# A three-block network on one core: norms, gated sums, head norms and HGRN levels written out anew between the matmul stages

## The reference, cut to what matters

```python
def rmsnorm(x, w):
    y = x32 * lax.rsqrt(jnp.mean(x32 * x32, axis=-1, keepdims=True) + EPS)
    return (y * w.astype(jnp.float32)).astype(x.dtype)

def second_block(...):                      # NSA, then FoX
        h = rms_norm(x, norm_g[i, 0])
        x = x + rms_norm(m, norm_g[i, 1])
        h = rms_norm(x, norm_g[i, 2])
        x = x + rms_norm(squared_relu_mlp(h, mlp_w_up[i], mlp_w_down[i]), norm_g[i, 3])

def hgrn2_chunkwise(q, k, log_f, v):
        bc = jnp.cumsum(gc, axis=2)
        diff = bc[:, :, :, None, :] - bc[:, :, None, :, :]
        decay = jnp.exp(jnp.where(mask[:, :, None], diff, NEG))
        a = jnp.einsum('bhtd,bhsd,bhtsd->bhts', qc, kc, decay)
        o = (jnp.einsum('bhtd,bhdv->bhtv', qc * jnp.exp(bc), s_st)
             + jnp.einsum('bhts,bhsv->bhtv', a, vc))

def hgrn2_mixer(h, w_in, lb, norm_w, w_out):
    o = merge_heads(head_rmsnorm(o, norm_w)).astype(h.dtype) * jax.nn.silu(g)
    return o @ w_out

def third_block(...):                       # mLSTM, then HGRN
        x = x + gate1 * y                   # y: the mixer's output
        hn = rmsnorm(x, norm2_w[layer]) * (1 + scale2) + shift2
        x = x + gate2 * y                   # y: SwiGLU, then the experts
    return rmsnorm(x, final_norm_w)
```

## Time and profile before

| what | us |
|---|---|
| median of 3 runs (lowest, highest) | 3282.08 (3279.73, 3282.49) |
| the profiled execution | 3282.36 |
| its span, first to last instruction | 3280.6 |
| PE busy | 2953.2 (90%) |
| DVE busy | 2152.5 (66%) |
| ACT busy | 1558.9 (48%) |
| POOL busy | 103.0 (3%) |

### The profile page before, as it was taken

One profiled execution on the slowest core, in us unless ns is written; L12 is line 12 of the kernel. 1 busy time (PEld: TensorE's weight loads), 2 busy tenths in 40 slices (PEclk: granted clock), 3 DMA queues, 4 the chain that ended last, 5 costly groups with the idle time before them and its releaser, 6 DMA issues. The chain is left out here.

```text
span 3280.6 us, 48259 instructions
## 1 busy us (share of the span) xinstructions
PE 2953.2 (90%) x19343; PEld 2606.9 (79%) x19343; DVE 2152.5 (66%) x3308; ACT 1558.9 (48%) x2454; POOL 103.0 (3%) x131
## 2 busy tenths in 40 slices
PE   7897998899999997878989699888997679999997
PEld 6896876679999997647978599768986669999996
DVE  5456498666666665275664666666555858888887
ACT  3442313344444444264443544544344248787875
POOL 0000000000000000200000000000001200000000
PEclk9998999999999998888999899899998879999998
DMA  6443488765665554304434244424552049998894
GB/s 262 157 180 140 154 354 341 311 226 193 207 224 208 202 194 163 129 1 153 180 142 154 77 180 158 158 84 154 179 193 103 1 165 337 332 339 326 326 339 185
DMA packets 76827, 648.61 MB, mean 198 GB/s; under 512 B 6104, under 2 KB 31192, under 8 KB 34032
## 3 DMA queue, kind: packets, MB, share of 16 engines
q1 hardware_dynamic: 49584, 621.09, 50.7%
q10 hardware_dynamic: 27072, 25.17, 2.4%
HBM read 632.60 MB, written 13.63 MB: 197 GB/s over the span
## 5 line engine op out<-in xcount | busy, mean ns | idle before, releaser
L1190 PE MATMUL ps<-x_hi,up_hi 128*128 128x256 f32 x1632 | 461.1, 283 | 2.8 <-DVE up_lo L1281 2.7
L1193 PE MATMUL ps<-x_lo,up_hi 128*128 128x256 f32 x1632 | 460.1, 282 | 0.0
L1194 PE MATMUL ps<-x_hi,up_lo 128*128 128x256 f32 x1632 | 460.0, 282 | 0.0
L346 DVE TENSOR_TENSOR weight_lo<-ring,weight_hi 128x1024 fp32r<-128x1024 f32 x236 | 288.1, 1234 | 258.4 <-ACT weight_hi L339 250.4
L339 ACT ACTIVATE weight_hi<-ring 128x1024 fp32r<-128x1024 f32 x236 | 245.6, 1054 | 184.7 <-PE ps L516 119.2
L1286 DVE TENSOR_TENSOR down_lo<-ring,down_hi 128x1024 fp32r<-128x1024 f32 x182 | 222.8, 1224 | 166.1 <-ACT down_hi L1243 166.1
L1190 PEld LDWEIGHTS ps<-x_hi,up_hi 128*128 128x128 f32 x1632 | 311.9, 191 | 10.3 <-DVE up_lo L1281 3.4
L1193 PEld LDWEIGHTS ps<-x_lo,up_hi 128*128 128x128 f32 x1632 | 312.0, 191 | 6.8
L1194 PEld LDWEIGHTS ps<-x_hi,up_lo 128*128 128x128 f32 x1632 | 311.6, 191 | 0.0
L1243 ACT ACTIVATE down_hi<-ring 128x1024 fp32r<-128x1024 f32 x182 | 193.1, 1061 | 232.2 <-PE ps L1215 232.2
L494 PE MATMUL ps<-x_hi,weight_hi 128*128 128x256 f32 x1024 | 291.5, 285 | 8.8 <-DVE weight_lo L346 8.1
(11 more groups left out here) (517 smaller groups left out, 6345.1 us busy)
## 6 DMA issues: line engine op xcount, KB each, us to landing
ring<-in_stream SPq DMA_DIRECT2D x181, 2048.0 KB, 7.7
ring<-in_experts SPq DMA_DIRECT2D x121, 1536.0 KB, 8.6
ring<-in_stream SPq DMA_DIRECT2D x22, 1536.0 KB, 6.4
gates<-kept_gates ACTq DMA_DIRECT2D x12, 1024.0 KB, 8.8
kept_gates<-away_first ACTq DMA_DIRECT2D x8, 768.0 KB, 10.7
kept_gates<-away_last ACTq DMA_DIRECT2D x8, 768.0 KB, 9.3
params_mix<-in_mix SPq DMA_DIRECT2D x1, 3072.0 KB, 21.6
params_ln<-in_ln SPq DMA_DIRECT2D x2, 1024.0 KB, 5.4
```

The source lines that it names most:

```text
L346: dve.tensor_tensor(self.place(self.lo, b), self.raw(b), self.place(self.hi, b), ALU.subtract).then_inc(self.split, 1)
L1190: last = pe.matmul(out, hi[:, o:o + P], x_hi[:, k, :], start=(k == 0), stop=False)
L1193: pe.matmul(out, hi[:, o:o + P], x_lo[:, k, :], start=False, stop=False)
L1194: last = pe.matmul(out, lo[:, o:o + P], x_hi[:, k, :], start=False, stop=(k == DK - 1))
```

## The change

The pieces above are written anew.

- Layer norms: the sum of x comes out of the adding instruction, tile by tile; ScalarE sums the squares of the centred x (center) while VectorE multiplies (norm_rows). The parameters of the second one are loaded at the start of the feed-forward ahead of it, those of the last norm in the stage ahead of it. The second one also squares x for the next stage, so that the NSA projection no longer does.
- post_norm: VectorE multiplies y with the gain while ScalarE squares it, for the first 512 columns as soon as the first of the two chunks of a mixer's output projection is done, and one instruction then multiplies with the root and adds to x.
- add_gated behind a mixer works on the first 512 columns likewise, and squares x in halves.
- HeadNorm: the weight of the norm goes into the scale with which the transposed result is copied, so GpSimd no longer multiplies; VectorE works head by head, one product from PSUM to each tile, and splits the head before the last two; the weight blocks' low parts stand between them.
- hgrn2: logarithm and cumulative sum move ahead of the last chunks, and the decays of levels 0 and 1 and the scaling of level 0 go into the projection. Of levels 0, 1 and 2, ScalarE copies the results straight to their places (weight_far, and squares of 64 and 32 tokens), and TensorE streams at levels 1 and 2 only the query columns that are needed; levels from 3 on stream whole tiles and are placed by VectorE under a mask, as all were. GpSimd clears the halves that no level has written yet.
- The output is stored in two DMAs, tile by tile.
- The four PSUM banks of y are in the order tile, half (they were in the order half, tile).

```diff
--- x squares, layer norm (both)
-            act.activation(junk[:, t, :], x[:, t, :], ACT.Square, accum_out=x_squares[:, t:t + 1])
+        def mean_square(act, out, of, to):
+            return act.activation(out, of, ACT.Square, scale=D ** -0.5, accum_out=to)
+        def center(act, mean_ready, junk, squared):
+            for t in range(TT):
+                act.wait_ge(mean_ready, t + 1)
+                act.activation(junk(t), halves(x[:, t, :]), ACT.Square, bias=less_mean[:, t:t + 1],
+                               accum_out=squares[:, t, 0:1]).then_inc(squared, 1)
+        def norm_rows(dve, z, g, b, mean_ready, squared, var_ready, rstd_ready, weighed, normed):
+            for t in range(TT):
+                dve.wait_ge(mean_ready, t + 1)
+                dve.scalar_tensor_tensor(z[:, t, :], x[:, t, :], less_mean[:, t:t + 1], g, ALU.add, ALU.mult).then_inc(weighed, 1)
+                dve.wait_ge(squared, t + 1)
+                dve.tensor_scalar(spare[:, t:t + 1], squares[:, t, 0:1], 1.0 / D, LN_EPS, ALU.mult, ALU.add).then_inc(var_ready, 1)
+            for t in range(TT):
+                dve.wait_ge(weighed, t + 1)
+                dve.wait_ge(rstd_ready, t + 1)
+                dve.scalar_tensor_tensor(x[:, t, :], z[:, t, :], rstd[:, t:t + 1], b, ALU.mult, ALU.add).then_inc(normed, 1)
--- feed_forward(..., ahead=(buf_2[:], d["ln2"])); add_gated(gate(3), ahead=(buf_last[:], d["last"]))
+                    if ahead is not None:
+                        sp.dma_start(*ahead).then_inc(ahead_loaded, 16)
--- post_norm, VectorE
-                    variances(dve, squares, var_ready, squared)
+                        dve.wait_ge(n_ready, 1)
+                        dve.tensor_tensor(weighed_y[:, :, 0:WIDE], bank_n(0), spread(g[:, 0:WIDE], 1, TT), ALU.mult).then_inc(y_weighed, 1)
+                        dve.wait_ge(n_ready, 2)
+                    for t in (1, 0):
+                        if t == 0:
+                            dve.wait_ge(squared, 1)
+                            variance(dve, squares, 0, square_parts).then_inc(var_ready, 1)
...
                     for t in range(TT):
                         dve.wait_ge(rstd_ready, t + 1)
-                        if t > 0:
-                            dve.wait_ge(x_ready, t)
-                        dve.scalar_tensor_tensor(halves(scaled_y[:]), y_banks(t), rstd[:, t:t + 1], halves(g), ALU.mult,
-                                                 ALU.mult).then_inc(y_scaled, 1)
-                        dve.wait_ge(y_scaled, t + 1)
-                        dve.tensor_tensor(x[:, t, :], x[:, t, :], scaled_y[:], ALU.add).then_inc(x_ready, 1)
+                        dve.scalar_tensor_tensor(x[:, t, :], weighed_y[:, t, :], rstd[:, t:t + 1], x[:, t, :], ALU.mult,
+                                                 ALU.add).then_inc(x_ready, 1)
--- add_gated with a mixer, VectorE
+                        o = slice(0, WIDE)
+                        dve.wait_ge(n_ready, 1)
+                        dve.tensor_tensor(gated_y[:, :, o], bank_n(0), spread(gate[:, o], 1, TT), ALU.mult).then_inc(y_gated, 1)
+                        dve.wait_ge(y_gated, 1)
+                        dve.tensor_tensor(x[:, :, o], x[:, :, o], gated_y[:, :, o], ALU.add).then_inc(x_ready, 1)
+                        o = slice(WIDE, D)
                         dve.wait_ge(n_ready, 2)
+                        for t in range(TT): ...
--- HeadNorm
+                weights.low(dve, 1)
                 dve.wait_ge(self.rstd_ready, 1)
-                dve.tensor_tensor(heads(self.o[:]), heads(self.o[:]), spread(self.var[:], 3, P), ALU.mult).then_inc(self.normed, 1)
+                for h in range(HEADS_C + 2):
+                    if h < HEADS_C:
+                        o = slice(h * P, h * P + P)
+                        for t in range(TT):
+                            last = dve.scalar_tensor_tensor(self.o[:, t, o], ps[:, 4 + 2 * t + h // 4, h % 4 * P:h % 4 * P + P],
+                                                            self.var[:, t, h:h + 1], self.gate[:, t, o], ALU.mult, ALU.mult)
+                        last.then_inc(self.normed, 1)
+                    b = h - 2
+                    if b >= 0:
+                        dve.wait_ge(self.high_ready, b + 1)
+                        dve.scalar_tensor_tensor(self.parts[1][:, b, :], ps[:, b % 4, 0:TOKENS], col("head_w", self.first_w + b),
+                                                 self.parts[0][:, b, :], ALU.mult, ALU.subtract).then_inc(self.ready, 1)
+                        if b in (1, 3, 5):
+                            weights.low(dve, b // 2 + 2)
...
-                pool.tensor_tensor(self.gate[:], self.gate[:], spread(self.norm_w, 1, TT), ALU.mult).then_inc(self.weighed, 1)
--- hgrn2, VectorE in the projection
+                    step(last)
+                    keep(1)
+                    decays(dve, 0).then_inc(diff_ready, 1)
+                    weights.low(dve, 29)
+                    dve.wait_ge(exped, 1)
+                    scale_q(dve, 0)
+                    weights.low(dve, 30)
+                    scale_k(dve, 0).then_inc(scaled, 1)
+                    weights.low(dve, 31)
+                    keep(2)
+                    dve.wait_ge(scaled, 1)
+                    decays(dve, 1).then_inc(diff_ready, 1)
+                    weights.low(dve, 32)
+                    keep(3)
+                    pool.memset(k_dec[0][:, :, P:TOKENS], 0.0)
+                    pool.memset(q_dec[0][:, :, 0:P], 0.0)
--- hgrn2, the levels
+                        pool.memset(weight[:], 0.0).then_inc(zeroed, 1)
+                        pool.memset(split(q_dec[1][:], P // 2)[:, :, 0, :], 0.0)
+                        pool.memset(split(k_dec[1][:], P // 2)[:, :, 1, :], 0.0).then_inc(zeroed, 1)
+                            if n > PLAIN:
+                                place(n - 1)
+                                    for o in range(0, P, 2 * half):
+                                        last = act.activation(weight[o:o + half, t, 4 * b:4 * b + 4, o + half:o + 2 * half],
+                                                              got[o:o + half, :, o + half:o + 2 * half], ACT.Copy)
+                                    if 0 < n < 3:
+                                        out, q_t = (a.rearrange("p (g a w) -> p g a w", a=2, w=levels[n])[:, :, 1, :] for a in (out, q_t))
+                                    m = levels[1] if n == 1 else P
+                                    last = pe.matmul(out[0:m], k[:, h, s * P:s * P + m], q_t, start=True, stop=True)
--- the end
-                sp.dma_start(d["out"], x[:]).then_inc(stored, 16)
+                    for t in range(TT):
+                        sp.wait_ge(normed, t + 1)
+                        sp.dma_start(d["out"][:, t, :], x[:, t, :]).then_inc(stored, 16)
```

462 lines of the change are left out of this document (250 added, 212 removed).

## The result

The changed kernel takes 3249.14 us (median of four runs, 3247.82 to 3250.10) against 3281.54 for the kernel before on the same chip (3279.73 to 3282.49): a ratio of 0.990, 95% interval 0.9884 to 0.9919. The interval leaves out 1, so the gain of one per cent is clear of noise. 3249.5 was forecast, in a range of 3240 to 3262. The profiled execution took 3248.25 us, its span 3246.5 (before 3280.6).

What follows compares the result with a forecast made beforehand. TensorE is busy nine tenths of the span, so time is won only where it waits, at stage changes and in HGRN. Terms sum to -32.7 from 3282.36, giving 3249.7, median 0.28 lower: 3249.5 us, range 3240 to 3262.

Steps and rivals of the forecast that it cites:

- -1.9: First layer norm: TensorE's gap of 9.30 us falls to 7.3 as ScalarE squares beside VectorE; 1.9 us less.
- -5.4: Second layer norm: earlier parameter DMA and x squared in the same stage let the next weight split end 5.4 us sooner.
- -2.6: Gated sums behind two mixers: half-width operations and a half square cut 6.1 us to 3.4; 2.6 us less each.
- each post norm: Norms behind NSA and FoX: first half weighed and squared beside the second chunk's matmuls; 3.1 us less each.
- Rival 4: Norm stretches: fused products or accumulating sums 1 us slower than separate ones in each of eight, 3257 us; chance 0.08.
- The head norm: Two head norms: a loss of 1.5 us each from the order and root lock, plus 1.6 each from cold clock.
- Rival 1: Head norm doesn't lose: GpSimd's root isn't held up and transposes keep the clock up, 3243 us; chance 0.17.
- HGRN: Projection and levels: moved work stalls the projection but lets levels start sooner, weighted sum at 2586.4; 14.7 us less.
- Rival 2: HGRN's overfull projection costs more: each of the last seven blocks stalls another 1.2 us, 3258 us; chance 0.20.
- Rival 3: Broken work leaves TensorE at 1.2 GHz: 14 blocks cancel the gain, all 32 give 3326 us; chance 0.02.
- The clearings: Early clearings of q_dec and k_dec beside VectorE's scaling of x: a loss of 0.5 us, bounds 0 to 1.9.
- The tail: Last norm and output: parameters a stage earlier and the second output half with half the bytes; 2.5 us less.

Runs made afterwards that it cites:

- e3: Changed kernel, but in both head norms VectorE makes the first weight_lo behind its wait for GpSimd's root, not beside it: 3247.12 us (one run).
- e1: Changed kernel with only HGRN's projection and levels as before the change: 3262.57 us, ratio 0.9941.
- e9: Changed kernel, head norm order untouched, plus 70 unread transposes at the start of each of the two head norm stages: 3250.49 us (one run).
- e6: Changed kernel with the exchanges of e4 and e5 and e2's dense head norm order, first weight_lo before the root wait, six transpose banks: 3231.60 us.
- e10: Kernel of e6 with 72 unread transposes ahead of the first real one in each head norm: 3227.94 us, ratio 0.9835.
- e4: Changed kernel with the last weight block's high part ahead of the second exponential on ScalarE in HGRN's projection: 3245.94 us, ratio 0.9891.
- e5: Changed kernel, ScalarE taking level 2's exponential before the far-half copies and GpSimd clearing q_dec and k_dec halves only after the input splits: 3254.60 us (one time).
- e8: The changed kernel once more, nothing altered: 3251.24 us, ratio 0.9906.
- e2: Changed kernel with gate products beside the root, then root products in two halves and dense transposes in both head norms: 3243.05 us, ratio 0.9884.

## Why the prediction was right

**The bound, and the norms.** Every stage change was read as a chain of single instructions, and the chains came out as added up: -1.96 for -1.9, -5.3 for -5.4, -2.4 and -2.55 for -2.6. The largest miss is 0.4 for each post norm, the second root beside a fused product with inputs in SBUF. The prediction priced such a lock in the head norm, where e3 shows it, and overlooked it here, where no run takes the product away. No run undid these edits one by one either. e1, which keeps them all, is 18.6 us faster than the kernel before (3281.15 and 3262.57), where the ledger gives its edits 16.8. Rival 4 (accumulating and fused forms slower by 1 us a stretch) is out: 0.08 for an accumulator on VectorE, 1.28 for a fused product.

**The head norm.** It loses, as forecast, by 3.5 and 3.9 where 3.1 was said. The order, the lock on the root included, cost 2.2 and 2.9 until the first matmul (1.5 said; the lock in it was 0.90 for 1.2), and the cold start the rest, 1.3 and 1.0 (1.6 said): the matmuls ran 2.8 and 2.1 us at half clock. So the 3.1 said lies near the 3.5 measured with one part too small and the other too large. Five traces with this head norm end its stages 40.2 to 40.9 and 39.7 to 41.1 us after the squares, so both losses are known to about 1 us only. Rival 1, no loss, falls. The reason given for the clock was incomplete: the prediction held it to be low because of the gap and to stay low in broken work. e9 shows that broken work is enough by itself. Nor do show that dense transposes bring the clock up within 3.24 us, as the prediction reads them: in e6 sixteen dense ones needed 5.8 and 6.0. What the prediction didn't ask is whether the old large products with the norm's weight in the copies' scale would be better still. e6 and e10 show that they are, by 5 and 7 us in each of the two stages.

**HGRN.** The mechanism holds, its term is mis-sized: -14.7 was said, -12.1 came. Undoing it together with the clearings (+0.8) costs 11.2, where the ledger has 11.4. Three sizes make the difference. The projection ended 9.1 late, not 8.1. Its first stall is 0.78 at the tenth block, as forecast (0.7); the prediction named the last high part behind the second exponential, but not that the block behind such a stall is cold as well (4.62 for 3.01). e4 puts 4.6 on that one place. The first cycle took 7.73 for 6.75, because the table load and the far copies stood ahead of the exponential (e5: 6.73). The third took 7.54, where the decays (L2891) needed 1.94 beside GpSimd's last two mask instructions; no run separates the two. On paper the six cycles were also 0.2 to 0.5 too long: three of 6.75 and three of 7.1 to 7.2 are 41.6 to 41.9, not 42.1. And TensorE isn't out of the bound everywhere there: the 12.9 us from the eighth scaling to the weighted sum were run at a granted 0.87; the same piece took 11.5 at 1.00 (e8) and 14.3 at 0.76 (e5). Rival 2 had this mechanism at seven blocks of 1.2; one place carried half of it. Rival 3's lost clock is real as well, but in the first block or two of each head norm and the last of the projection, not in 14.

**The clearings**: +0.8 for +0.5, by the gap ahead of the transposes (6.14, 5.38 before, 5.52 in e5). The Trainium skill (SBUF — State Buffer, "Who interferes with whom") says that VectorE in a two-port mode, which a tensor_scalar can enter, contends with GpSimd, and that the one that comes second is blocked for the whole instruction of the first. The scaling's 2.20 beside the MEMSETs and 1.58 without them agree.

**The tail**: -3.1 for -2.5. The last product waits 0.83 for its root and no longer for parameters (the earlier trace rows has 2.85):

```profile
3240.84 2.48 DVE L3644 SCALAR_TENSOR_TENSOR x<-x,rstd,params_last 128x1024 f32<-128x1024 f32 x2 [0.83 <-POOL rstd L567]
3242.15 1.54 SPq L3651 DMA_DIRECT2D out<-x  x2
```

**The sum.** The median came 0.4 us from the forecast, and that is luck. The edits' own stretches give 28.2 where 32.7 was said: 4.5 short, in HGRN, the post norms and the head norms. Drift in untouched stretches made it up in this pair of traces (5.9). The medians say 32.4 and, in e8, 31.3. Whether the 3 to 4 us between are chance alone stays open: of the kernel before there is one trace, and its NSA stretch, less the norm's 5.3, lies at 229.3, near the long end of the eleven.

## What to carry to other kernels

Between two dense stages add up the chain instruction by instruction. At the norms and gated sums here it came out within half a microsecond each, and what it missed most was a GpSimd instruction that nobody had checked for what VectorE does beside it. Filling a slack with moved work costs where a piece that TensorE needs next stands behind a piece that nobody needs yet: look for that one instruction in each queue before giving up on the fill. And don't break up TensorE's short work to start it earlier: dense, with the idle time ahead filled by transposes that nobody reads, was 7 us better in each head norm.

## What the runs showed of the hardware

- TensorE's granted clock can fall while it works: after 70 dense transposes at 1.00, transposes in pairs (busy 2.19 of 4.55 us, then 2.08 of 4.10) were granted 1.00 and then 0.51.
- From the first transpose of a head norm to full clock it took, with 16 dense ones, 3.2 and 3.4 us in the kernel before and 5.8 and 6.0 in e6; 8.2 and 7.3 with a pause of 0.8 in them (e2); and 10.6 to 13.6 in pairs (changed kernel, e1, e3, e4, e5, e8).
- GpSimd's power of 128 x 16 took 2.91 us alone and 3.81 beside a VectorE TENSOR_TENSOR of 1.22 with both inputs in SBUF.
- An untouched stretch of 224 us (NSA) came out at 224.0 to 230.5 in eleven traces of changed kernels. The granted clock in the 11 us ahead of its longest gap was 0.69 or 0.85 in the three that took 230.4 to 230.5, and 1.00 in the eight that took 224.0 to 227.3.
